# Full attention by two heads at a time: where maxima and gate steps stand, who adds a head's two weight sums, and how many value products stand in a row

## The reference, cut to what matters

```python
s = jnp.einsum('bkgqd,bksd->bkgqs', q_blk, kt).astype(jnp.float32) * scale
p = jax.nn.softmax(s, axis=-1).astype(vt.dtype)
return jnp.einsum('bkgqs,bksd->bkgqd', p, vt)
```

## Time and profile before

| | us |
|---|---|
| median of 3 runs | 1983.53 |
| lowest, highest | 1982.91, 1988.68 |
| the profiled execution's own time | 1981.81 |
| its span, first to last instruction | 1980.0 |

### The profile page before, as it was taken

How to read it: one execution, slowest core, us unless ns; L and a number is a source line. 1 busy time by engine, 2 the same in 40 slices (tenths; PEclk the granted TensorE clock), 3 DMA queues, 4 the chain that set the end, 5 groups by cost and what they waited for, 6 DMA issues and landing times.

```text
span 1980.0 us, 23931 instructions
## 1 busy us (share of the span) xinstructions
PE 1906.8 (96%) x8908; PEld 1472.0 (74%) x8908; DVE 1201.3 (61%) x1766; ACT 894.5 (45%) x1507; POOL 186.1 (9%) x284
## 2 busy tenths in 40 slices
PE   6999998999889999999999999999999999999898
PEld 4778884445687778888888788887888887776587
DVE  7795857655575787677555546656453455445754
ACT  6542344555453552332333434434523666355752
POOL 1101104333100000111000100000012000000000
PEclk9999999999999999999999999999999999999999
DMA  8426416785505413455211653334442000005052
GB/s 330 159 97 220 176 50 115 124 172 101 149 1 184 171 72 127 144 175 202 79 60 54 219 206 123 112 122 144 160 138 75 33 33 33 22 26 189 0 182 95
DMA packets 80978, 241.33 MB, mean 122 GB/s; under 512 B 9808, under 2 KB 15056, under 8 KB 80608
## 3 DMA queue, kind: packets, MB, share of 16 engines
q1 hardware_dynamic: 47168, 141.15, 20.0%
q0 software_dynamic: 33696, 98.65, 17.8%
HBM read 177.30 MB, written 34.61 MB: 107 GB/s over the span
## 4 chain that ended last, share of the span: by engine, by line
PE 81%; DVE 9%; DMA 4%; ACT 3%; issue 3%; SPq 0%; DVEq 0%; POOL 0%; ACTq 0%; POOLq 0%
PE ps L1369 13%; PE ps L1371 13%; PE ps L1370 13%; PE ps L1693 6%; PE ps L1695 6%; PE ps L1694 6%; PE ps L1524 4%; PE ps L1496 3%; PE ps L1519 3%; PE ps L1498 2%; DMA x_scratch<-x 2%; PE ps L1460 1%; DVE mh L2480 1%; DMA w_raw<-in_weights 1%; DVE w_lo L2348 1%
## 5 line engine op out<-in xcount | busy, mean ns | idle before, releaser
L1369 PE MATMUL ps<-h_hi,w_hi 128*128 128x512 f32 x832 | 334.5, 402 | 10.0 <-DVE h_lo L2348 6.6
L1371 PE MATMUL ps<-h_hi,w_lo 128*128 128x512 f32 x832 | 325.8, 392 | 0.0
L1370 PE MATMUL ps<-h_lo,w_hi 128*128 128x512 f32 x832 | 325.4, 391 | 0.0
L2348 DVE TENSOR_TENSOR w_lo<-w_raw,w_hi 128x1024 fp32r<-128x1024 f32 x139 | 170.0, 1224 | 238.2 <-ACT w_hi L1860 236.6
L1860 ACT ACTIVATE w_hi<-w_raw 128x1024 fp32r<-128x1024 f32 x140 | 147.6, 1056 | 242.6 <-DMA w_raw<-in_weights 242.2
L2480 DVE TENSOR_REDUCE mh<-ps 128x1 f32<-128x512 f32 (+1 forms) x224 | 137.4, 630 | 120.6 <-PE ps L1460 46.5
L1369 PEld LDWEIGHTS ps<-h_hi,w_hi 128*128 128x128 f32 x832 | 157.8, 190 | 45.1 <-DVE h_lo L2348 7.9
L1371 PEld LDWEIGHTS ps<-h_hi,w_lo 128*128 128x128 f32 x832 | 156.9, 189 | 34.0
L1370 PEld LDWEIGHTS ps<-h_lo,w_hi 128*128 128x128 f32 x832 | 157.2, 189 | 32.0 <-issue 1.4
L1369 PE MATMUL ps<-hid_hi,w_hi 128*128 128x512 f32 x352 | 138.0, 392 | 4.7 <-DVE hid_kept_lo L2348 2.4
L1693 PE MATMUL ps<-t_hi,pair_S_r 128*128 128x512 f32 x352 | 137.9, 392 | 4.4 <-DVE pair_S_r L2348 2.6
(11 more groups left out here) (412 smaller groups left out, 3869.1 us busy)
## 6 DMA issues: line engine op xcount, KB each, us to landing
w_raw<-in_weights SPq DMA_DIRECT2D x140, 512.0 KB, 3.6
p_sums<-full_pf POOLq DMA_DIRECT2D x96, 256.0 KB, 4.1
ada_next<-in_ada POOLq DMA_DIRECT2D x32, 512.0 KB, 5.0
ada_last<-in_ada POOLq DMA_DIRECT2D x24, 512.0 KB, 5.2
pair_gate<-in_weights SPq DMA_DIRECT2D x22, 512.0 KB, 3.5
pair_up<-in_weights SPq DMA_DIRECT2D x22, 512.0 KB, 4.5
ada_first<-in_ada SPq DMA_DIRECT2D x8, 1024.0 KB, 17.7
m_scratch<-y POOLq DMA_DIRECT2D x12, 512.0 KB, 5.4
```

Source lines behind the costliest of these rows:

```text
L1369: e.matmul(o, w_hi[slot][:, tile_of(kw)], hi, start=start, stop=False, skip_group_check=skip)
L1370: e.matmul(o, w_hi[slot][:, tile_of(kw)], lo, start=False, stop=False, skip_group_check=skip)
L1371: return e.matmul(o, w_lo[slot][:, tile_of(kw)], hi, start=False, stop=stop, skip_group_check=skip)
L2348: return e.tensor_tensor(dst, src, hi.bitcast(F32), ALU.subtract)
```

## The change

- `V_GROUP` is 4 instead of 2: value products are issued for four units at a time.
- The maxima of a pair end six units ahead of the next pair instead of four, so 16 maxima stand in units 1 to 10.
- The gate parts 1 to 4 move to units -12, -10, -8 and -6; parts 5 to 18 move into units 11 to 15 of a pair.
- The sums of a pair move from step 2 to step 8 of the next pair. For the first seven pairs a new step `pjoin`, at step 3, lets POOL add a head's second sum tile to its first, and PE then multiplies only one tile for each head.
- The counters q_cp and q_lo become one counter q_made.

```diff
-V_GROUP = 2
+V_GROUP = 4
...
-        low, high = (starts[m - 1] + 1, start - 4) if m else (-4 - len(steps), -4)
+        low, high = (starts[m - 1] + 1, start - 6) if m else (-4 - len(steps), -4)
...
         if i % 2 and g == last[i]:
-            ended.append((g + 3, job))
+            ended.append((g + 9, job))
+        if ended and ended[0][0] == g + 5:
+            p.add("pjoin", *ended[0][1])
         if ended and ended[0][0] == g:
             p.add("dsum", *ended[0][1])
...
-    for part, g in enumerate((-14, -11, -8, -5, 3, 7, 14, 15, 30, 31, 46, 47, 62, 63, 78, 79, 86, 87, 95)):
+    for part, g in enumerate((-14, -12, -10, -8, -6, 11, 13, 15, 27, 29, 31, 43, 45, 47, 59, 61, 63, 75, 79)):
...
-                    e.wait_ge(s["q_cp"], job_no(kind, h, n) + 1)
+                    e.wait_ge(s["q_made"], 2 * job_no(kind, h, n) + 1)
...
-                    e.wait_ge(s["q_lo"], job_no(kind, h, n) + 1)
+                    e.wait_ge(s["q_made"], 2 * job_no(kind, h, n) + 2)
...
-                for part in range(2):
+                pair = take_no(kind, h, n)
+                joined = pair < FULL_TAKES - 1
+                if joined:
+                    e.wait_ge(s["p_join"], 2 * pair + 2)
+                for part in range(1 if joined else 2):
                     for odd in range(2):
-                        e.wait_ge(*summed(kind, h - 1 + odd, n, KT - 2 + part))
-                        x = e.matmul(ps[rows_of(odd), bank, :], ones[:, 0:64], sums_of_pair(take_no(kind, h, n))[2 * odd + part][:, :], start=part == 0, stop=part == 1,
-                                     skip_group_check=True)
+                        if not joined:
+                            e.wait_ge(*summed(kind, h - 1 + odd, n, KT - 2 + part))
+                        x = e.matmul(ps[rows_of(odd), bank, :], ones[:, 0:64], sums_of_pair(pair)[2 * odd + part][:, :], start=part == 0,
+                                     stop=joined or part == 1, skip_group_check=True)
...
+            def join_sums(kind, h, n):
+                sums = sums_of_pair(take_no(kind, h, n))
+                for odd in range(2):
+                    for u in (KT - 2, KT - 1):
+                        e.wait_ge(*summed(kind, h - 1 + odd, n, u))
+                    total = sums[2 * odd][:, :]
+                    e.tensor_tensor(total, total, sums[2 * odd + 1][:, :], ALU.add).then_inc(s["p_join"], 1)
```

More of the change, by code:

```diff
@@ L97 @@
     "half_mm y_out pad_made conv_taps conv_out m_kept m_in o_in rope_in qk_sq side_mm side_out qk_r qk_step qk_rot "
-    "at_set vt aux kk_hi kk_made q_hi q_cp q_lo mx_mm mcol rowt row sink_f sink_h sink_l sink_mm "
-    "sc p_exp p_sum0 p_sum1 p_sum2 p_sum3 val den_mm inv div "
+    "at_set vt aux kk_hi kk_made q_hi q_made mx_mm mcol rowt row sink_f sink_h sink_l sink_mm "
+    "sc p_exp p_sum0 p_sum1 p_sum2 p_sum3 p_join val den_mm inv div "
     "sel_in g_act g_vec g_tr g_cols st_hi st_lo sel_made sums_one k_tr k_made v_tr v_made m_mm e_made s_mm wgt wr_mm qp_made "
@@ L2460, in q_copy @@
                 e.wait_ge(*q_ready(kind, h, n))
-                e.tensor_copy(AB[kind].qq[q_buffer(kind, h, n)][rows_of(1 - h), :], q_src(kind, h, n)).then_inc(s["q_cp"], 1)
+                e.tensor_copy(AB[kind].qq[q_buffer(kind, h, n)][rows_of(1 - h), :], q_src(kind, h, n)).then_inc(s["q_made"], 1)
             def q_low(kind, h, n):
@@ L2467, in q_low @@
                 to = A.qq[b][rows_of(h), :] if kind == "fox" else A.qa[b][0:64, :]
-                low_part(to, q_src(kind, h, n), A.qq[b][rows_of(h), :]).then_inc(s["q_lo"], 1)
+                low_part(to, q_src(kind, h, n), A.qq[b][rows_of(h), :]).then_inc(s["q_made"], 1)
             def max_unit(kind, h, n, u):
@@ L3055, in y_tile @@
                     e.dma_start(out_half[k - 1:k + 1].rearrange("k p t -> p k t"), yo[:, k - 1:k + 1, :]).then_inc(s["out0"], 16)
-            work = {"psum": weight_sum, "yt": y_tile, "start": start, "condl": condition, "adal": ada_load, "rtab": rope_tables, "keep": keep, "keep_x1": keep_x1, "hk": keep_hid, "hl": load_hid,
+            work = {"psum": weight_sum, "pjoin": join_sums, "yt": y_tile, "start": start, "condl": condition, "adal": ada_load, "rtab": rope_tables, "keep": keep, "keep_x1": keep_x1, "hk": keep_hid, "hl": load_hid,
                     "ft": final_normed, "y2": keep_z, "gaterows": gate_rows, "spill": spill, "set3": set3}
```

## The result

The changed kernel takes 1989.71 us (median of 20 runs, 1983.04 to 1997.55) against 1983.61 for the kernel before (20 runs, 1981.21 to 1988.68): ratio 1.0029, 95% interval 1.0019 to 1.0038. The prediction said 1974.5, a range from 1964 to 1985 and a chance of 0.11 for slower; it was wrong by 15.2 us, in the wrong direction. The profiled execution took 1986.94, with a span of 1985.1.

What follows compares the result with a forecast made beforehand. It held that in the changed stretch PE is paced by switches between kinds of matmul and by waits: 20.1 us saved, 11.2 given back, 8.9 less than 1981.81, plus 1.7 to the median, gives 1974.5; range 1964 to 1985.

Steps and rivals of the forecast that it cites:

- the value groups: Value products on PE: 64 groups become 32, each saving a 0.33 us width round trip, 10.6 us; lower bound 0.
- the last units: From unit 102, with two score banks, third scores wait for exponentials: 0.5 on each of six groups, 3.0 us given back.
- The 0.93 at the first row stays: First head's maximum row: PE's 0.93 us wait for DVE remains, two maxima again being issued just ahead of it.
- Gate steps: Gate parts on DVE moved behind the maxima: 3.5 us saved, 1.2 given back for parts 3 and 4.
- part 3 at -8: Gate parts 3 and 4 near the projection's end: one stall of 1.2 us given back, bounds 0 and 3.5.
- The join: POOL adds each head's two sums in 7 pairs: 6.0 us saved on PE, 1.5 given back for held query copies.
- the 9 us worked out from that rule: DVE beside POOL's additions: if blocked at both additions in every pair, 7 x 1.3 = 9 us lost instead of 1.5.
- The rival built on it: Slower: additions of 3.0 us hold DVE's query copy and the maxima behind it, 1988 to 2008 us; chance 0.11.
- Crowded maxima: Steps 1 to 4 of a pair: sixth and seventh maximum wait about 0.3 us each for DVE, 4.2 us given back.
- the marks that I named: Eight-record groups of 1.94 us, 36 sum records, sums 23 to 23.5 apart, first-pair row waits within 1.1, additions 1 to 1.6.

Runs made afterwards that it cites:

- b_v4: The kernel before with V_GROUP 4 and nothing else of the change; ratio 1.0008 to the kernel before.
- a_v2: The changed kernel with V_GROUP 2 again; 1977.83 us, ratio 0.9970 to the kernel before.
- the fills: The changed kernel with 32 or 18 small unused matmuls on PE ahead of the rows at units 30 and 103; ratios 1.0026 and 1.0037 to the kernel before.
- a_max4: The changed kernel with the maxima ending four units ahead of the next pair, as before; ratio 1.0009 to the kernel before.
- d_gates: The changed kernel with V_GROUP 2 and gate parts 8 to 12 at units 27, 31, 43, 47 and 59; 1977.73 us, ratio 0.9967 to the kernel before.
- a_nojoin: The changed kernel without POOL's additions, PE multiplying both sum tiles of each head at step 8; ratio 1.0041 to the kernel before.
- a_rows: The changed kernel with both maximum rows of pairs 1 to 7 moved, first two steps later, second two earlier; ratio 1.0065 to the kernel before.
- a_rowb: The changed kernel with only the second head's maximum row moved, four units ahead of the next pair instead of two; ratio 1.0078 to the kernel before.
- c_gates: The changed kernel with V_GROUP 2 and gate parts 8 to 12 at units 31, 43, 44, 45 and 46; 1977.70 us, ratio 0.9958 to the kernel before.

## Why the prediction was wrong

- **The step that failed is the value groups**: "ACT needs 0.595 for each against a longer step of PE, so in the stretch with three score banks I take all of it", 10.6 us, less 3.0 for the last units. Measured, groups of four lose where 7.6 us were to be gained: 1.6 us in the kernel before (b_v4), 12 us in the changed kernel (against a_v2), where the first row and the crowded maxima now stand so that groups of two would have covered them. The size of one switch was right (1.87 us for a group of four against 2 x 1.01 for two of two, with 0.2 around each: 0.35 saved, 0.33 forecast). What I did not ask is what the removed value group had covered. I asked only whether the exponentials would be there, and not what else lay behind a group: DVE's reductions before the first row (0.93 in each pair, none with groups of two), ACT's writing of the second row (0.59), the memory's key products ahead of the row at unit 103 (2.06 against 1.03), the sums' own switch. Of the 3.0 for the last units, which I had for third scores that wait for exponentials, the trace shows 1.1 (0.21 and 0.90). "The 0.93 at the first row stays" counted a loss that groups of two would have removed.
- **The clock was in no term and no rival.** The earlier trace rows show 1.00, and the 2.17 wait of the earlier trace rows had no fall behind it. From that I took full speed for granted. By the slope, some 5 of the 12 us between a_v2 and the changed kernel go with the clock (0.9947 against 0.9912), which would leave 7 for waits. This split is a relation, not an experiment, and the fills, which raised the clock and gained nothing clear, do not support it. Shown is the whole, 12 us; how it divides stays open.
- **Gate steps.** I forecast 3.5 saved and 1.2 given back; undoing them changes nothing (1.0026 against 1.0029). "The later ones stand in steps 11 to 15, where DVE has no maxima" was true, and missed that the second row stands in step 14: parts 8 and 9 at 27 and 29 are ahead of it. With groups of two they still cost a wait of 2.14 there (2.49 with four). Of the 1.2 for part 3 at -8 the trace shows 0.95 (a maximum at 290.88).
- **The join** was right: some 4 us with groups of two (4.5 forecast), 2.4 with groups of four, additions of 1.26 to 1.57 us (1.3 taken). The Trainium skill ("SBUF — State Buffer", Who interferes with whom) has the second of two fully blocked; the casts of 1.55, 0.79, 0.62 and 0.56, each over 0.27 to 0.29 after the addition that was running, agree. But a cast met an addition in four pairs only, and mostly near its end, so the 9 us worked out from that rule did not come: PE waited 1.10, 0.34 and 0.18. With groups of two (a_v2) casts took up to 0.91 us, and no wait of PE for a maximum stands behind them. The rival built on it is not what made the kernel slower.
- **Crowded maxima** were right with groups of four (4.2 forecast, 4 measured by a_max4), and nothing with groups of two.
- **The sum.** By its own terms the forecast is 1974.6, not 1974.5. All but the value groups was forecast at 1.3 us less (8.9 less 7.6) and came to 6 (a_v2). The value groups are off by 19. Together 14.6, which is the way from the forecast's 8.9 less to the 5.7 more of the ratio. This split takes the groups out last; the parts depend on each other, as b_v4 and a_max4 show.
- Of the marks that I named, the records (8 of 1.94, 36 of the sums), additions of 1 to 1.6 us and no wait over 1.1 us at the first pair's rows (0.94 and 0.64) came. The pairs of 23.2 us did not, and a wait of 2.49 came in the second pair, at unit 30, for which I had named no mark. That d_gates has pairs of 23.2 us is luck: they come from the join and from a first row that no longer waits, not from groups of four.

## What to carry to other kernels

Before work on the busiest engine is gathered into larger groups, list what each group covers: every wait that now is short because a group lies between issue and need. The saving per switch was right to a few per cent, and the cover was worth more. When a step is moved behind one queue, read what stands ahead of it in the queue it comes to: three of my own mends (a_rows, a_rowb, c_gates) moved a pause instead of removing it.

## What the runs showed of the hardware

- In the traces of the changed kernel and of the experiments, between 300 and 515 us, there are 46 stretches at 1.2 GHz, each of 3.4, 6.8 or 10.2 us. 31 began at a pause of PE of 1.3 us or more, or behind one (29 soon, two only after 8 and 9 us); ahead of the others the waits were shorter or none. Nor does every pause bring one: counted with the kernel before, 18 of 20 pauses of 2.0 us or more were followed by a fall, and 11 of 34 from 1.3 to 2.0 us. The 2.17 us of the earlier trace rows is one of the two long ones without. Filling two pauses took their falls away. The Trainium skill ("TensorE: Matmul & The Clock Gate", What's actually happening) says that the clock has only two levels and that activity releases the lower one; the traces agree, at 0.51 over 348 to 355 us.
- The spread of a kernel's times goes with the clock: the changed kernel's runs with a clock of 0.988 took 1994.0 to 1997.6 us, those with 0.994 took 1983.0 and 1988.1.
- Additions of 128x512 on POOL took 1.28 us (median of 14). A DVE cast of 0.42 that came while one ran took up to 1.55 and ended 0.27 to 0.29 after it; in the traces without additions (before, a_nojoin) all 12 casts of the stage took 0.42.
